# Two layers written out one behind the other, with the first layer's row tiles read from the inputs ahead of constants, weights and clearings

## The reference

```python
for l in range(DEPTH):
    xn = _rms(xp, norm_pre[l])
    mix_a, mix_b, mix_c, mix_d, gates = _project(xn, w_in[l], fox_bias[l], lbs[l], log_gamma, pos_p)
    o_a, st_a = _gla_prompt(*mix_a)          # gated recurrence
    o_b = _fox_prompt(q_b, k_b, v_b, lf_b)   # forgetting attention
    o_c = _dsa_prompt(q_c, k_c, v_c, iq_c, ik_c, iw_c)   # top-k sparse attention, with an indexer
    o_d, st_d = _gla_prompt(*mix_d)          # retention
    xp = xp + _merge(o_a, o_b, o_c, o_d, gates, w_out[l], norm_post[l])
    # the same for xs, the running stream, with caches and states
```

## Time and profile before

| | |
|---|---|
| time, median of 3 runs | 2138.87 us (2136.68 to 2142.58) |
| the profiled execution: time | 2146.08 us |
| the profiled execution: span | 2144.4 us |
| mean granted TensorE clock | 0.982 of full speed |
| PE busy | 1932.9 us (90%) |
| DVE busy | 1392.8 us (65%) |
| ACT busy | 736.3 us (34%) |
| POOL busy | 259.0 us (12%) |

### The profile page before, as it was taken

One profiled execution on the slowest core, in us unless ns is written; L12 is line 12 of the kernel. 1 busy time (PEld: TensorE's weight loads), 2 busy tenths in 40 slices (PEclk: granted clock), 3 DMA queues, 4 the chain that ended last, 5 costly groups with the idle time before them and its releaser, 6 DMA issues. The chain is left out here.

```text
span 2144.4 us, 27310 instructions
## 1 busy us (share of the span) xinstructions
PE 1932.9 (90%) x9670; PEld 1083.1 (51%) x9690; DVE 1392.8 (65%) x2961; ACT 736.3 (34%) x1678; POOL 259.0 (12%) x360
## 2 busy tenths in 40 slices
PE   3999999989999788999959999999899988889997
PEld 2634457555545555654444344565554455565443
DVE  3268488998796776533233684989897956665322
ACT  3353134233212544443243512334331134444332
POOL 0000132342100000001100002233221000000011
PEclk9999999999999999999979999999999999999998
DMA  8201214121323003223351022221205130022242
GB/s 281 99 25 67 79 47 136 61 81 50 113 73 77 18 6 94 89 67 132 128 193 55 25 71 74 92 97 60 96 30 153 38 72 13 26 76 87 95 149 103
DMA packets 151272, 178.34 MB, mean 83 GB/s; under 512 B 71408, under 2 KB 106736, under 8 KB 150864
## 3 DMA queue, kind: packets, MB, share of 16 engines
q1 hardware_dynamic: 123072, 139.19, 20.7%
q10 hardware_dynamic: 28064, 37.38, 4.9%
HBM read 119.72 MB, written 66.69 MB: 87 GB/s over the span
## 5 line engine op out<-in xcount | busy, mean ns | idle before, releaser
L914 PE MATMUL ps<-wring,xnT_arena 128*128 128x512 f32 (+2 forms) x2304 | 921.3, 542 | 0.0
L914 PEld LDWEIGHTS ps<-wring,xnT_arena 128*128 128x128 f32 x2304 | 405.0, 192 | 354.5 <-issue 337.7
L1759 DVE TENSOR_SCALAR_CACHE_REDUCE arena<-arena,theta 32x1056 bf16<-32x1056 f32 x496 | 461.3, 979 | 2.3
L1396 ACT COPY arena<-ps 128x512 f32<-128x512 f32 (+3 forms) x144 | 75.3, 523 | 449.4 <-PE ps L914 415.8
L1274 PE MATMUL ps<-wring,xnT_arena 128*128 128x512 f32 x512 | 223.9, 595 | 0.0
L2043 DVE TENSOR_REDUCE mneg<-ps 128x1 f32<-128x192 f32 (+9 forms) x148 | 113.9, 770 | 87.1 <-PE ps L1206 84.7
L1274 PEld LDWEIGHTS ps<-wring,xnT_arena 128*128 128x128 f32 x512 | 96.4, 191 | 115.4 <-issue 115.4
L1050 PEld LDWEIGHTS ps<-arena 128*128 128x128 f32 x488 | 69.6, 193 | 106.8 <-DVE arena L1866 78.2
L2206 POOL TENSOR_TENSOR arena<-arena 128x1024 f32<-128x1024 f32 (+1 forms) x16 | 35.5, 2216 | 727.2 <-DVE arena L1984 539.1
L1050 PE MATMUL ps<-arena 128*128 128x128 f32 x488 | 80.2, 287 | 39.5 <-DVE arena L1866 39.3
L1361 ACT COPY xnT_arena<-ps 128x512 f32<-128x512 f32 (+3 forms) x84 | 39.0, 464 | 188.9 <-PE ps L1218 141.6
(11 more groups left out here) (270 smaller groups left out, 2495.1 us busy)
## 6 DMA issues: line engine op xcount, KB each, us to landing
projected<-arena ACTq DMA_DIRECT2D x130, 256.0 KB, 2.0
arena<-residual SPq DMA_DIRECT2D x34, 512.0 KB, 5.2
wring<-in_w_in SPq DMA_DIRECT2D x16, 1024.0 KB, 7.6
o_bc<-projected SPq DMA_DIRECT2D x36, 384.0 KB, 3.7
wring<-in_w_in SPq DMA_DIRECT2D x6, 2048.0 KB, 8.8
wring<-in_w_out SPq DMA_DIRECT2D x8, 1024.0 KB, 5.5
residual<-arena SPq DMA_DIRECT2D x16, 512.0 KB, 2.6
out<-arena SPq DMA_DIRECT2D x16, 512.0 KB, 4.0
```

The costliest lines, as they stand in the source:

```text
L914: o = mm(bank(pbank(k), 0, w_), xnT[:, c, t * P:(t + 1) * P], w, start=(c == 0), stop=(c == CH - 1))
L1396: nc.scalar.copy(stage[s][:, 0:wide], bank(pbank(k), 0, wide)).then_inc(p_ev, 1)
L1759: V.tensor_scalar(cmp_out[0][r, (i % 2) * WMAX:(i % 2) * WMAX + uw[u]], score[u][r], th_, 0.0, op, ALU.add, accum_out=into[r, i:i + 1]).th ...
```

## The change

The register loop becomes a Python loop: the block is written twice, one copy behind the other, with constant addresses. In the first copy (layer 0) row tiles 1 to 8 come straight from x_prompt, in the opening and in the output loop, and tile 0 is put together in `xl[0]` (and later in `XR[0]`) from x_sample and meta_tokens over a memset. The prologue keeps only the first 130 columns of `cf` (the identity and two scalars), that memset and the two small loads. The other constants, their casts, and the clearings move into layer 0's block; new waits stand in front of their readers. The nine row tiles are issued ahead of all of them.

```diff
-                sp.dma_start(cf[:, :], cf_d).then_inc(ld_const, 16)
-                sp.dma_start(arena[:, D:D + cb_d.shape[1]], cb_d).then_inc(ld_const, 16)
...
-                sp.dma_start(res_d[P:3 * P], x_prompt[0, 0:2 * P]).then_inc(ld_init, 16)
+                sp.dma_start(cf[:, 0:FIRST], cf_d[:, 0:FIRST]).then_inc(ld_first, 16)
                 sp.wait_ge(dve_own, 1)
...
-                sp.dma_start(res_d[3 * P:], x_prompt[0, 2 * P:]).then_inc(ld_rest, 16)
-                sp.wait_ge(dve_own, 3)
-                sp.dma_start(prj_d[HALF:P], o_bc[0:HALF].rearrange("p t n -> p (t n)")[:, 0:N_IN]).then_inc(ld_rest, 16)
-                sp.wait_ge(ld_const, 64)
-                sp.wait_ge(ld_init, 80)
+                sp.dma_start(xl[0][0:NS], x_sample[0]).then_inc(ld_init, 16)
+                sp.dma_start(xl[0][SMETA:HALF], meta_tokens).then_inc(ld_init, 16)
...
-                nc.vector.memset(arena[0:HALF, 0:D], 0.0).then_inc(dve_own, 1)
+                nc.vector.memset(xl[0], 0.0).then_inc(dve_own, 1)
                 nc.vector.memset(lbsel[:, :], 0.0).then_inc(dve_own, 1)
-                nc.vector.memset(o_bc[:, :, :], 0.0).then_inc(dve_own, 1)
...
-        with nc.Fori(0, DEPTH) as layer:
-            at_layer = bass.ds(layer, 1)
+        for layer in range(DEPTH):
+            at_layer = slice(layer, layer + 1)
+            source = (lambda t: x_prompt[0, (t - 1) * P:t * P]) if layer == 0 else (lambda t: res_t[t])
...
-                        if t == 3:
-                            sp.wait_ge(ld_rest, 32)
-                        sp.dma_start(xl[t % 2], res_t[t]).then_inc(ld_x[ld_x_slot[t]], 16)
+                        if layer > 0 or t > 0:
+                            sp.dma_start(xl[t % 2], source(t)).then_inc(ld_x[ld_x_slot[t]], 16)
...
                     for t in range(4, NT):
                         x_tile(t)
+                    if layer == 0:
+                        sp.dma_start(cf[:, FIRST:], cf_d[:, FIRST:]).then_inc(ld_const, 16)
...
                     w_group(1)
+                    if layer == 0:
+                        sp.wait_ge(z_clear, 1)
+                        sp.dma_start(res_d[HALF:P], o_bc[0:HALF].rearrange("p t n -> p (t n)")[:, 0:D]).then_inc(ld_rest, 16)
+                        sp.dma_start(prj_d[HALF:P], o_bc[0:HALF].rearrange("p t n -> p (t n)")[:, 0:N_IN]).then_inc(ld_rest, 16)
...
+                            sp.wait_ge(xr_clear, 1)
...
                     pe.wait_ge(i_rep, 1)
+                    pe.wait_ge(ld_const, 64)
+                    if layer == 0:
+                        pe.wait_ge(ld_rest, 32)
...
+                        if t == 6 and layer == 0:
+                            V.memset(o_bc[:, :, :], 0.0).then_inc(z_clear, 1)
...
+                    dve.wait_ge(ld_const, 64)
+                    if layer == 0:
+                        V.tensor_copy(cb[:, :], arena[:, D:D + cb_d.shape[1]]).then_inc(cast, 1)
+                        V.tensor_copy(cm[:, :], arena[:, 2 * D:2 * D + cm_d.shape[1]]).then_inc(cast, 1)
...
+                    if layer == 0:
+                        pool.wait_ge(a_pv, a_pv_at["fox", UNIT_GROUPS[-1][0], 1])
+                        nc.gpsimd.memset(XR[0][:, 0:512], 0.0).then_inc(xr_clear, 1)
+                        pool.wait_ge(ld_first_res, 32)
```

More of the change, by code:

```diff
@@ L89, in constants @@
     f["ident"] = np.eye(P)
+    f["eps"] = np.full((P, 1), EPS)
+    f["one"] = np.ones((P, 1))
     for v, same in ((0, same0), (1, np.ones((P, P), bool))):
@@ L114, in constants @@
     f["live"] = ((r % HALF < 32) | (r % HALF >= SMETA))[:, None]
-    f["eps"] = np.full((P, 1), EPS)
-    f["one"] = np.ones((P, 1))
     units = [SW] + [width(t) for t in range(2, NT)]
@@ L387, in encoder @@
         FKS = [k for k in KSL if k[0] == "fox"]
-        ld_rest = sem("ld_rest")
-        ld_const, ld_init, ld_layer = sem("ld_const"), sem("ld_init"), sem("ld_layer")
+        ld_first, ld_const, ld_init = sem("ld_first"), sem("ld_const"), sem("ld_init")
+        ld_rest, ld_layer = sem("ld_rest"), sem("ld_layer")
+        z_clear, xr_clear, cast = sem("z_clear"), sem("xr_clear"), sem("cast")
+        FIRST = cf_at["one"][1]
         ld_gpre = sem("ld_gpre")
@@ L580, in encoder @@
         ld_res = [sem(f"ld_res{i}") for i in range(3)]
+        ld_first_res = sem("ld_first_res")
         ld_res_slot, ld_res_at = ring(T_all, len(ld_res))
@@ L689, in _, with loaded @@
                 nc.vector.memset(lbsel[:, :], 0.0).then_inc(dve_own, 1)
-                nc.vector.memset(o_bc[:, :, :], 0.0).then_inc(dve_own, 1)
-                dve.wait_ge(ld_const, 64)
-                nc.vector.tensor_copy(cb[:, :], arena[:, D:D + cb_d.shape[1]]).then_inc(dve_own, 1)
-                nc.vector.tensor_copy(cm[:, :], arena[:, 2 * D:2 * D + cm_d.shape[1]]).then_inc(dve_own, 1)
         nc.all_engine_barrier(sems_to_clear=range(ids[0], ids[-1] + 1))
-        with nc.Fori(0, DEPTH) as layer:
-            at_layer = bass.ds(layer, 1)
+        for layer in range(DEPTH):
+            at_layer = slice(layer, layer + 1)
+            source = (lambda t: x_prompt[0, (t - 1) * P:t * P]) if layer == 0 else (lambda t: res_t[t])
+            def loaded(eng, t):
+                if layer == 0 and t == 0:
+                    eng.wait_ge(ld_init, 32)
+                else:
+                    eng.wait_ge(ld_x[ld_x_slot[t]], ld_x_at[t] - (16 if layer == 0 and ld_x_slot[t] == ld_x_slot[0] else 0))
@@ L752, in _ @@
                     sp.wait_ge(st_idx, 48)
+                    if layer == 0:
+                        sp.wait_ge(ld_rest, 32)
                     mix_loads(0)
@@ L842, in res_loads @@
                     def res_loads(t):
-                        if t == 0:
+                        if t == 0 and layer == 0:
+                            sp.wait_ge(xr_clear, 1)
+                            for half in range(2):
+                                c = slice(512 * half, 512 * (half + 1))
+                                sp.dma_start(XR[0][HALF * half:HALF * half + NS, 0:512], x_sample[0, :, c]).then_inc(ld_first_res, 16)
+                                sp.dma_start(XR[0][HALF * half + SMETA:HALF * (half + 1), 0:512], meta_tokens[:, c]).then_inc(ld_res[0], 16)
+                        elif t == 0:
                             for half in range(2):
@@ L921, in first_group @@
                         project(0, t, jobs[t - 3] if t >= 3 else None)
+                    pe.wait_ge(ld_first, 16)
                     for t in T_all:
@@ L2079, in _ @@
                     pool.wait_ge(idx_clear, 1)
+                    pool.wait_ge(ld_const, 64)
                     G = nc.gpsimd
```

16 lines of the change are left out of this document (7 added, 9 removed).

## The result

The changed kernel takes 2107.39 us in the median of 4 runs (2105.63 to 2113.13), beside 2138.28 us in the median of 4 runs of the kernel before (2136.68 to 2142.58). The ratio is 0.9857 (95% interval 0.9837 to 0.9876), so 30.9 us (26.5 to 34.9) are gone. The forecast was 2117, with a range from 2111 to 2126: right in sign and in the places named, and 9 us short, outside the range. The profiled execution took 2108.83 us, with a span of 2107.0 and a mean granted clock of 0.988.

What follows compares the result with a forecast made beforehand. PE's own work, 90% of the span, was taken as the bound and unchanged; only its idle start and layer turn could move. Gains of 20.8 + 0.8 + 0.3 = 21.9 us from 2138.87 gave 2117 us, range 2111 to 2126.

Steps and rivals of the forecast that it cites:

- Layer 0's opening: Start to index phase: an earlier barrier and shorter load queue bring the index phase to 62.5 from 83.34, 20.8 us gained.
- Two signs: Opening of layer 0: PE's first transposes were to stand at 10 to 12 us, the third at 18 to 20.
- Moved DVE work at nothing: Layer 0 before the index phase: the moved 3.90 us memset and the casts of 0.55 and 0.69 cost nothing.
- The output loop of layer 0: Layer 0's stores: two more DMA issues and a memset on SP's path, covered by thirty microseconds, cost 0.
- Turn and exit: Layer 0 to layer 1 and the loop's end: 0.8 us gained at the turn, some 0.3 at the exit.
- Rival B: Before the index phase: PE waits for the moved transfers, costing up to 8.7 us, 2119 to 2126; chance 0.18.
- C: Opening: bound by loads after all, each row tile late, gain mostly given back, about 2130 us; chance 0.07.
- D: Whole kernel: twice the code makes the instruction stream slower, 2145 us or more; chance 0.05.
- Sum: 20.8 + 0.8 + 0.3 = 21.9 us: Whole kernel: opening, turn and loop exit add to 21.9 us gained, all other parts at 0.
- gaps that grow: Inside the layers: the prediction was to count as failed if PE's gaps there grew.
- The way from trace to median: Whole kernel: differences taken from the profiled execution, 7.2 us above the median, are applied to the median of 2138.87.

Runs made afterwards that it cites:

- order_alone: The kernel before with only `eps` and `one` moved behind the identity in `cf`, other tables two columns further on: 2133.15 us against 2139.76, ratio 0.9966.
- table_stride: The kernel before with the cosine and sine rows of a row tile 33 columns apart instead of 32: 2140.64 us in one run.

## Why the prediction was right and where it failed

- **Layer 0's opening: right.** 20.8 us forecast, 21.5 in the trace, 22.1 by the difference of ratios. Its steps held: block at 4.2 (4.5 forecast), third transposes at 17.49 (18.9), index phase 61.81 (62.5), constants landed at 44.9 (45.2), `w_group(1)` at 50.2 (50.8), clearing at 53.6 (54.3). The surplus is at the front: row tile 2 was there at 14.4, not 15.8. Two signs fell just outside what the forecast named, PE's first transposes at 9.90 (10 to 12) and the third at 17.49 (18 to 20), both on the early side. The constants in the block are 2587 KB and not 2652, since 65 KB of `cf` came in the prologue, 0.2 us at the forecast's own rate.
- **Moved DVE work at nothing: right**, by the unchanged 44 us from the third transposes on. The output loop of layer 0 shows no cost either: from SP's next load to its last store it takes 148.6 us (900.51 to 1049.07), before 148.7.
- **Turn and exit: right**, 1.4 us in the trace for 1.1, 2.8 (0.4 to 5.1) in the experiment.
- **Rival B: did not occur**, yet the forecast priced the clearings by bytes alone, at 2.7 us each 1003 KB where 4.9 were measured one behind the other. That they landed as forecast (3.5 us behind `w_group(1)` forecast, 3.4 measured) was luck: the forecast had them wait for it, and they moved beside it. **Rivals C and D: did not occur**, by the unchanged 44 us for C and by the 1.72 MB of the two instruction queues for D.
- **The step that failed: "Sum: 20.8 + 0.8 + 0.3 = 21.9 us".** The sum has no term for the order of the tables in `cf`. Of the inside of the layers the forecast took only that PE's work stays as it is, named gaps that grow as a sign of failure, and gave no price to tables that move by two columns. The gaps shrank, and two falls of the clock went with them: 6.9 us by rows, 7.3 (4.1 to 10.5) measured alone. With it the sum is 21.5 + 1.4 + 6.9 = 29.8 us, within 26.5 to 34.9; the parts measured apart give 22.1 + 2.8 + 7.3 = 32.2 beside 33.0 for the whole in the same comparison as the 22.1.
- **The way from trace to median: right.** Differences were applied to the median and not to the profiled execution. The spans differ by more, 37.4 us, because that one execution was 7 us above its median, at a clock of 0.982.

Shown by experiment: the place of two columns is the cause of the missing term (added alone, and taken away alone), and the slow places repeat every four columns. Shown in rows, of the two kernels and order_alone: the chain from POOL through DVE to PE; in all thirteen traces: the wait and the clock at this place. Not shown: why POOL reads a row slower from those places, and whether the clock at this place would fall for another reason; table_stride's layer 0, 1.92 us idle with no fall, warns that the wait's length is not all.

## What to carry to other kernels

When a diff changes the layout of a packed constant tensor, list every reader of it, and look in the trace for the same instruction at other offsets: a POOL operation on a repeated short row had two durations 15% apart, by the column at which the row starts. An engine busy for 12% of the time can set the pace if the operations of a fuller engine stretch beside its own: look for rows of one form with two durations and see what runs beside the long one. And in an opening bound by loads, what counts is which bytes stand ahead of the first ones needed, and which waits stand ahead of the barrier.

## What the runs showed that was not expected

- POOL's 128x512 product with a row of 32 floats repeated 16 times: 1.12 us from a row whose first column leaves 1 or 2 over a multiple of four, 1.29 from one that leaves 0 or 3; the 128x256 product with `gq`: 0.94 us at 2 against 1.03 at 0.
- PE's clock at 1.2 GHz for some 3.4 us behind a wait of 1.90 us and not behind one of 1.55, at the same place of both layers, which made 0.35 us of DVE's lateness into 0.96 us from row to row. One wait of 1.92 us had no fall.
- Clearing 1003 KB from 64 partitions took 4.9 us, 210 GB/s, when such clearings stood one behind the other.
- The mean granted clock of one kernel's executions varied from 0.981 to 0.990, and its time by 15 us.
